# Last stage of a decoder step: every first output tile of two is multiplied in 64-row halves of TensorE into two banks

## What is computed

```python
def conv_glu(n, conv_prev, w_up, conv_w, conv_b, w_down):
    gate, up = _split(n @ w_up, (D_FF, D_FF))
    ...
    return (jax.nn.silu(c) * up) @ w_down, ext[:, T:]
...
    f, conv_new = conv_glu(rmsnorm(h, norm2), conv_prev, w_up, conv_w, conv_b, w_down)
    return h + f, ...
...
y_prompt = rmsnorm(hp, norm_f)
```

## Time and profile before

| | |
|---|---|
| median of 3 runs | 1795.07 us (1794.8 to 1795.44) |
| the profiled execution | 1794.71 us, its span 1793.1 us |
| TensorE busy | 1772.1 us, 99% of the span |
| VectorE busy | 1118.7 us, 62% |
| ScalarE busy | 756.2 us, 42% |
| mean granted TensorE clock | 0.998 of full speed |

### The profile page before, as it was taken

The page is one execution under the profiler, slowest core; times in us unless marked ns, Lnnn a source line. Parts: engine busy times, 40 slices in busy tenths (PEclk is TensorE's granted clock), DMA queues, the critical chain, the costliest instruction groups (busy, mean ns, idle before and its releaser), DMA issues.

```text
span 1793.1 us, 40756 instructions
## 1 busy us (share of the span) xinstructions
PE 1772.1 (99%) x16532; PEld 1713.3 (96%) x16532; DVE 1118.7 (62%) x1989; ACT 756.2 (42%) x1049; POOL 53.8 (3%) x103
## 2 busy tenths in 40 slices
PE   9999999999999999999999999999999999999997
PEld 8999899988888888999999999999999999999996
DVE  7764954667777777766556666666666665444444
ACT  6566444544444444533443333333333333333332
POOL 2500000000000000000000000000000000000000
PEclk9999999999999999999999999999999999999999
DMA  7644344422223322644455444444444444555543
GB/s 287 229 163 150 131 159 148 156 102 102 105 105 110 110 105 106 221 165 153 169 203 181 169 158 170 160 167 160 168 158 171 160 168 162 174 175 171 172 167 133
DMA packets 51552, 283.45 MB, mean 158 GB/s; under 512 B 7232, under 2 KB 11840, under 8 KB 25632
## 3 DMA queue, kind: packets, MB, share of 16 engines
q1 hardware_dynamic: 43632, 260.61, 40.8%
q10 hardware_dynamic: 3600, 12.29, 1.9%
q0 software_dynamic: 4256, 9.65, 1.7%
HBM read 274.25 MB, written 8.27 MB: 158 GB/s over the span
## 4 chain that ended last, share of the span: by engine, by line
PE 95%; DVE 3%; ACT 1%; DMA 1%; issue 0%; DVEq 0%; SPq 0%; ACTq 0%
PE bank L618 29%; PE bank L620 28%; PE bank L619 28%; PE bank L954 1%; PE bank L993 1%; DVE w_lo L564 1%; DMA w_raw<-in_w_in 1%; DVE scores L1914 1%; PE bank L1052 0%; PE bank L859 0%; PE bank L913 0%; PE bank L807 0%; PE bank L824 0%; DVE max L1881 0%; PE bank L639 0%
## 5 line engine op out<-in xcount | busy, mean ns | idle before, releaser
L618 PE MATMUL bank<-x_split,w_lo 128*128 128x288 f32 x2880 | 873.0, 303 | 0.0
L619 PE MATMUL bank<-x_split,w_hi 128*128 128x288 f32 x2880 | 849.5, 295 | 0.0
L620 PE MATMUL bank<-x_split,w_hi 128*128 128x288 f32 x2880 | 846.9, 294 | 0.0
L584 ACT ACTIVATE w_hi<-w_raw 128x2048 fp32r<-128x2048 f32 (+1 forms) x262 | 468.9, 1790 | 591.6 <-PE bank L620 572.3
L564 DVE TENSOR_TENSOR w_lo<-w_raw,w_hi 128x2048 fp32r<-128x2048 f32 (+1 forms) x238 | 504.0, 2117 | 286.1 <-ACT w_hi L584 285.7
L618 PEld LDWEIGHTS bank<-x_split,w_lo 128*128 128x128 f32 x2880 | 539.8, 187 | 17.4 <-issue 9.5
L619 PEld LDWEIGHTS bank<-x_split,w_hi 128*128 128x128 f32 x2880 | 541.0, 188 | 1.8 <-issue 0.7
L620 PEld LDWEIGHTS bank<-x_split,w_hi 128*128 128x128 f32 x2880 | 542.1, 188 | 0.0
L618 PE MATMUL bank<-act_split,w_lo 128*128 128x288 f32 x704 | 208.5, 296 | 0.0
L619 PE MATMUL bank<-act_split,w_hi 128*128 128x288 f32 x704 | 207.7, 295 | 0.0
L620 PE MATMUL bank<-act_split,w_hi 128*128 128x288 f32 x704 | 207.0, 294 | 0.0
(11 more groups left out here) (390 smaller groups left out, 1558.8 us busy)
## 6 DMA issues: line engine op xcount, KB each, us to landing
w_raw<-in_w_up SPq DMA_DIRECT2D x88, 1024.0 KB, 4.7
w_raw<-in_w_in SPq DMA_DIRECT2D x47, 1024.0 KB, 4.8
w_raw<-in_w_down SPq DMA_DIRECT2D x64, 704.0 KB, 4.0
w_raw<-in_w_gate SPq DMA_DIRECT2D x32, 1024.0 KB, 4.8
w_raw<-in_w_p SPq DMA_DIRECT2D x16, 1024.0 KB, 4.8
w_raw<-in_w_o SPq DMA_DIRECT2D x16, 1024.0 KB, 4.8
h<-in_x ACTq DMA_DIRECT2D x1, 2304.0 KB, 12.0
h_spill<-h ACTq DMA_DIRECT2D x1, 2304.0 KB, 9.3
```

The source lines that it names most:

```text
L584: actv(WHI[:, slot, 0:kt], WRAW[:, slot, 0:kt], ACT.Copy).then_inc(sem("w_hi"), 3 if isinstance(n, int) and n == 2 else 1)
L618: mm(out, wl, hi, start=first and k == ks[0], stop=False, skip_group_check=True)
L619: mm(out, w, lo, start=False, stop=False, skip_group_check=True)
L620: ins = mm(out, w, hi, start=False, stop=last and k == ks[-1], skip_group_check=True)
```

## The change

In the last stage the units of tile 0 of each group call a new helper, `row_halves`, in place of `blocks`. Each product of 128 rows of depth becomes two products of 64 rows: the upper 64 partitions of weights and activations are multiplied into bank 0, the lower 64 into bank 2. The order of the three kinds of product is kept, upper half and lower half alternate. Tile 1 is made as before, in bank 1. When tile 0 is done, VectorE adds bank 2 to the residual, waits for its own addition, and adds bank 0. VectorE's loop over the groups goes through a helper that counts those waits (`st.repeat`); its body is otherwise the same.

```diff
+            def row_halves(slot, out, rhs, first, last, k_from):
+
+                for k in range(DK):
+                    hi, lo, w, wl = rhs[:, 0, k_from + k], rhs[:, 1, k_from + k], WHI[:, slot, k], WLO[:, slot, k]
+                    for i, (st, mv) in enumerate(((wl, hi), (w, lo), (w, hi))):
+                        for x, r in enumerate((slice(0, 64), slice(64, 128))):
+                            ins = mm(out[x], st[r], mv[r], start=first and k + i == 0,
+                                     stop=last and (k, i) == (DK - 1, 2), skip_group_check=True)
+                return ins
...
-                    blocks(n, j % 2, range(DK), BK[tile][:, 0:N], XF, q == 0, q == DU - 1,
-                           k_from=q * DK).then_inc(sem("unit_done"), 1)
+                    if tile:
+                        ins = blocks(n, j % 2, range(DK), BK[1][:, 0:N], XF, q == 0, q == DU - 1, k_from=q * DK)
+                    else:
+                        ins = row_halves(j % 2, (BK[0][:, 0:N], BK[2][:, 0:N]), XF, q == 0, q == DU - 1, q * DK)
+                    ins.then_inc(sem("unit_done"), 1)
...
+                        if tile == 0:
+                            st.done(V.tensor_tensor(t, t, BK[2][:, 0:N], ALU.add))
                         V.tensor_tensor(t, t, BK[tile][:, 0:N], ALU.add).then_inc(sem("down_out"), 1)
...
-            with dve.Fori(1, KT // 2 - 1) as g:
-                down_units(g)
+            st.repeat(KT // 2 - 1, 1, down_units, first=1)
```

## The result

The kernel after takes 1796.88 us (median of 20 runs, 1795.92 to 1798.05), the kernel before 1793.91 us in the runs beside them (1793.17 to 1795.44). The ratio is 1.0015, with a 95% interval from 1.0009 to 1.0022: about 3 us more. The whole interval lies above 1, so the change is slower beyond the noise of twenty runs each, though its middle, 0.15%, is less than the 0.2% up to which the prediction counted a difference as none. The profiled execution's span grew from 1793.1 us to 1795.8.

A forecast was written before the change was run, and what follows sets the result against it. The prediction took the pace of TensorE's products as the bound. Its terms, 0 (pairs) + 3.2 (changes of shape) + 0 (feeding TensorE) + 0 (VectorE), on the median of 1795.07 gave 1798.3 us, range 1786 to 1814.

The forecast's parts named there:

- The pair: Last stage, tile 0: two half products together cost what one whole product costs, 0.1333 us.
- The term of 0: Tile 0's 1056 products turned into pairs of halves at an unchanged 0.1333 us each add 0 us.
- The changes of shape: TensorE going from whole products to halves and back, 8 times in the last stage: 8 x 0.395 = 3.2 us.
- The forecast's second figure: Line 730 with 256 columns: 1.10 us less 0.133 + 0.43 + 0.133 of work leaves 0.40 us lost.
- its two pieces: Loss on the way in: 0.09 us after the columns are through and a bare 0.11 us load; same on way back.
- VectorE and issue: Second addition of 0.46 us at tile 0's end, and TensorE's doubled instructions in those units: cost 0 each.
- 0.83 us of cover: Gap on VectorE after tile 0's addition, while `w_lo` waits for ScalarE's `w_hi`; the second addition fits in it.
- The level: Forecast time of 1798.3 us, set on the three-run median of 1795.07 for the kernel before, 0.18% more.
- A: Rival: halves in tile 0 lose less than whole products, pair at 0.1225 us, 1786.9 us in all; chance 0.14.
- B: Rival: each pair in tile 0 pays a little more, 1803.1 to 1817.3 us in all; chance 0.15.
- C: Rival: halves in tile 0 take turns, pair at 0.22 to 0.267 us, 1890 to 1939 us; chance 0.13.
- the likeliest case: Pairs cost nothing extra, shape changes 3.2 us: 1798.3 us, from 1796 to 1800.5; chance 0.55, 0.37 of it within 0.2%.

The follow-up runs named there:

- four quarters: Against the kernel before: tile 0 in four parts of 32 rows, into four banks, with four additions at its end; 1796.4 us, ratio 1.0014.
- three by three: As the change, but per depth tile the three upper products come first, then the three lower; 1796.98 us, beside 1793.93 before.
- 33 by 33: As the change, but in each unit of tile 0 all 33 upper products come first, then all 33 lower; 1913.39 us, ratio 1.0665 to before.

## Why the prediction was right, step by step

**The pair.** The term of 0 holds: 0.133 us on the timeline, and 1.00 within the interval when all tiles go in halves. The row that decided it, line 730, was plain f32 at half the pace; the doubt was whether two halves also go together at full pace, and they do, as do four quarters.

**The changes of shape.** Forecast 0.395 us a round trip, 3.2 in all; the timeline shows 0.19 a change, 0.38 a round, 16 x 0.19 = 3.0, and the medians differ by 2.97. The number of changes, 2, 16, 32 and 320 in four kernels, orders their times, and the last gives 0.19 us each again. The forecast's second figure, 0.40 with 256 columns, was no independent check: its 0.43 of work was found by taking the first step's 0.11 and 0.09 off, which then count as lost. And at line 730 the number type changes along with the shape; here the type stays the same, and 0.38 against 0.39 leaves it next to no part. That its two pieces are the emptying and a load with nothing over it is read from the rows (the earlier trace rows and those after); no run took one of them away.

**VectorE and issue.** Both at no cost, as forecast: the second addition left 0.35 us of the 0.83 us of cover, and even four additions cost nothing. Quarters doubled the number of instructions once more and kept the pace.

**The level.** The forecast of 1798.3 stood on a median of three runs, 1795.07; twenty runs put before at 1793.91, so the level is off by 1.2 us and the step by 0.2.

**The rivals.** A is out by the equal pace of tile 0 and tile 1, 0.133 us at 288 columns and 0.119 at 256. B is out: the second half rides along free. C is out: no pair takes turns. The Trainium skill's rule behind A ("TensorE: Matmul & The Clock Gate", Part 3, The mechanism: loads overlap products only on other row groups) is not borne out, since in a train of whole products the load begins with a product on the same rows and the step of 0.133 gains nothing from halves. The Trainium skill's 4 ns per further tile (same page, Measured speedup vs the span model) is not paid per pair in a train: in quarters it would be 1056 x 0.012 = 12.7 us by that figure, an estimate, and the run shows 2.5 in all. I had given the slower side 0.46, more than the same at 0.40: 0.28 of it for B and C, which did not come, and 0.18 for the upper part of the likeliest case. What was measured lies in the lower part of that case, below 0.2%, to which I had given 0.37, the highest chance of all.

## What to carry to other kernels

Splitting a product into row halves gains nothing when all rows are already filled: the halves run together, but each takes the step of a whole product. What it costs is the way in and out, 0.19 us each time here, so count the changes of shape, not the split products, and keep products of one shape together. For products with only 64 rows of depth the same runs say the opposite: put two of them side by side on the two halves, in the order of the program at most about three products apart, and the second is free.

## What was not expected of the hardware

TensorE started products out of the order of the program when their rows were free, about three products ahead at each change of halves: three by three is as fast as one by one, 33 by 33 loses most of the sharing, 119.4 us of the 141 that two products in turn would cost.

With 128 moving columns the granted clock fell from 1.00, 2.4 GHz, to 0.50, 1.2 GHz, some 5 us into the stage, after a wait of 0.56 us for `w_lo` near 1500.76, and it did not rise again though TensorE's rows show no gap from then on. Windows of that kernel:

```profile
1496.50:1499.50 3.00, 3.00 (x58) 3.00 (x56) 2.05 (x4) 2.21 (x2) 0.00 (x0) 1.00 0.86 337
1502.00:1504.00 2.00, 2.00 (x24) 2.00 (x22) 1.43 (x1) 0.00 (x0) 0.00 (x0) 0.50 1.03 379
1600.00:1700.00 100.00, 100.00 (x731) 99.53 (x731) 25.80 (x24) 22.99 (x23) 0.00 (x0) 0.50 0.33 107
```

At that level a pair takes two times as long (three from 1559.60 to 1560.24, 0.21 us each, against 0.11), and fewer columns cost more time than they saved. This is one execution; what made the clock fall and what kept it low was not tried.
